# Leaving out the identity matmuls between the products of the level loop in the RWKV scan of a two-layer hybrid backbone

## What is computed

```python
def rwkv7_scan(inputs, s0):
    def step(S, xs):
        r, w, k, v, a, b = xs
        sa = jnp.einsum('bhvk,bhk->bhv', S, a)
        S = S * w[:, :, None, :] + sa[..., None] * b[:, :, None, :] + v[..., None] * k[:, :, None, :]
        return S, jnp.einsum('bhvk,bhk->bhv', S, r)
    return lax.scan(step, s0, inputs)
```

## Time and profile before

| | |
|---|---|
| median of 3 runs | 6901.06 us (6895.18 to 6903.48) |
| span of the profiled execution | 6891.5 us |
| TensorE busy | 4825.8 us (70%) |
| VectorE busy | 4673.2 us (68%) |
| ScalarE busy | 1084.8 us (16%) |
| GpSimd busy | 1818.5 us (26%) |
| RWKV scan, 12 chunks | 839.7 us |

### The profile page before, as it was taken

One profiled execution on the slowest core, in us unless ns is written; L12 is line 12 of the kernel. 1 busy time (PEld: TensorE's weight loads), 2 busy tenths in 40 slices (PEclk: granted clock), 3 DMA queues, 4 the chain that ended last, 5 costly groups with the idle time before them and its releaser, 6 DMA issues.

```text
span 6891.5 us, 63224 instructions
## 1 busy us (share of the span) xinstructions
PE 4825.8 (70%) x17384; PEld 2626.8 (38%) x17384; DVE 4673.2 (68%) x11232; ACT 1084.8 (16%) x2298; POOL 1818.5 (26%) x2660
## 2 busy tenths in 40 slices
PE   8898877869555555555555789987787855555554
PEld 3698454636111111111111269954464411111111
DVE  1554154545999999999987354415463699999977
ACT  1100032211111111111111110002221111111111
POOL 0000000000444444444456100000000144444454
PEclk9899887789677767676777889998768966667777
DMA  5000100001999999999999600000001399999998
GB/s 203 13 1 1 37 10 22 10 25 58 381 390 361 392 362 390 358 392 354 391 375 420 255 22 1 1 31 11 27 7 40 126 389 359 390 371 378 390 390 363
DMA packets 221384, 1463.98 MB, mean 212 GB/s; under 512 B 24593, under 2 KB 28945, under 8 KB 57233
## 3 DMA queue, kind: packets, MB, share of 16 engines
q0 software_dynamic: 184320, 1342.26, 49.0%
q1 hardware_dynamic: 30848, 113.20, 4.6%
q10 hardware_dynamic: 6032, 6.05, 0.3%
HBM read 1459.31 MB, written 2.10 MB: 212 GB/s over the span
## 4 chain that ended last, share of the span: by engine, by line
DVE 43%; PE 36%; issue 11%; DMA 5%; ACT 2%; POOL 1%; DVEq 1%; POOLq 0%; ACTq 0%; SPq 0%
PE psum L335 36%; DVE arena L1511 11%; DVE u_features L1511 7%; DVE arena L1162 5%; DMA arena<-in_uv,arena 4%; DVE arena L1036 3%; DVE psum L1520 2%; DVE arena L1517 1%; DVE arena L1161 1%; DVE arena L1316 1%; DVE arena L1197 1%; DVE arena L1389 1%; DVE arena L1045 1%; DVE arena L1039 1%; DVE arena L1194 1%
## 5 line engine op out<-in xcount | busy, mean ns | idle before, releaser
L335 PE MATMUL psum<-arena,lora_weights 128*128 128x512 f32 (+2 forms) x1968 | 1465.9, 889 | 1026.1 <-ACT lora_weights L970 992.0
L335 PEld LDWEIGHTS psum<-arena,lora_weights 128*128 128x128 f32 (+1 forms) x1968 | 465.8, 261 | 2042.4 <-ACT lora_weights L970 1612.6
L1511 DVE CUSTOM_DVE_ANT_0 arena<-arena,y_features 128x1024 f32<-128x1024 f32 x800 | 957.6, 1221 | 70.4 <-DMA arena<-in_uv,arena 70.4
L335 PE MATMUL psum<-arena 128*128 128x64 f32 (+5 forms) x7136 | 969.6, 315 | 46.9 <-DVE arena L1316 23.8
L1023 POOL DMA_INDIRECT arena<-in_uv,arena x800 | 829.0, 1036 | 239.3 <-issue 212.3
L335 PEld LDWEIGHTS psum<-arena 128*128 128x128 f32 (+2 forms) x7136 | 829.8, 213 | 129.0 <-ACT arena L894 28.8
L335 PE MATMUL psum<-u_features,lora_weights 128*128 128x512 f32 x640 | 512.7, 947 | 484.6 <-ACT lora_weights L970 482.3
L335 PE MATMUL psum<-u_features,weight_ring 128*128 128x256 f32 (+1 forms) x2368 | 782.3, 493 | 16.5 <-DVE u_features L1042 11.6
L1018 POOL COPY arena<-arena 128x2 uint32 x640 | 246.7, 385 | 1753.7 <-PE psum L335 1655.7
L1511 DVE CUSTOM_DVE_ANT_0 u_features<-u_features,y_features 128x1024 f32<-128x1024 f32 x480 | 575.6, 1219 | 23.6 <-DMA u_features<-in_uv,arena 20.8
L335 PEld LDWEIGHTS psum<-u_features,weight_ring 128*128 128x128 f32 x2368 | 458.4, 194 | 326.2 <-issue 272.6
(11 more groups left out here) (187 smaller groups left out, 5013.7 us busy)
## 6 DMA issues: line engine op xcount, KB each, us to landing
weight_ring<-in_ws SPq DMA_DIRECT2D x202, 512.0 KB, 3.3
arena<-in_uv,arena POOLq DMA_INDIRECT x800, 9.6
u_features<-in_uv,arena POOLq DMA_INDIRECT x480
arena<-in_ln ACTq DMA_DIRECT2D x8, 512.0 KB, 4.9
x_tokens<-in_x SPq DMA_DIRECT2D x1, 2048.0 KB, 13.2
out_x<-x_tokens SPq DMA_DIRECT2D x1, 2048.0 KB, 6.6
consts<-in_cf SPq DMA_DIRECT2D x1, 1674.0 KB, 6.8
x_tokens<-in_ctx SPq DMA_DIRECT2D x1, 1024.0 KB, 8.9
```

What stands on the lines that cost most here:

```text
L335: return pe.matmul(o, w, x, start=first, stop=last, skip_group_check=True)
L1511: dve.tensor_tensor_reduce(out=GB[s][:, 0:D], in0=GB[s][:, 0:D], in1=u, scale=1.0, scalar=0.0, op0=ALU.mult, op1=ALU.add, accum_out=DOT[:, ...
```

## The change

The constant WARM goes from 3 to 0:

```diff
-WARM = 3
+WARM = 0
```

## The result

The changed kernel takes 7088.44 us (median of 4 runs, 7066.28 to 7101.42), the kernel before 6898.12 in the same sessions (6890.65 to 6903.48). The ratio is 1.0269, with a 95% interval from 1.0249 to 1.0289: slower by 2.7%. Forecast were 7080 us and 2.6%. The profiled execution spans 7085.7 us against 6891.5, 194.2 us more.

What follows compares the result with a forecast made beforehand. TensorE was taken to bound the RWKV scan, with its clock deciding the sign: +19.9 us in each of ten chunks (+199), -20 for two last chunks, +179 on 6891.5 gives 7070, plus 9.6 makes 7080 us; range 6980 to 7190.

Steps and rivals of the forecast that it cites:

- up to level 1: RWKV chunks with preparation, level 0 up to the start of level 1's "dT": starts earlier, -2.0 us per chunk.
- level 2: Same chunks: wait unchanged at 3.58 us, "dT" between full and half clock, +1.6 us as the middle of 0 and 3.2.
- levels 3, 4, 5: Same chunks: products at half clock, 10.1 us per level instead of 6.7, +3.4 each, +10.2 us per chunk.
- level 6 and the chunk's end: Same chunks: level 6 with the last group +1.1 us; W, U and out partly at half clock, +9 us.
- The pause: Between levels 1 and 2, TensorE's idle time before "dT" grows from 0.24 to 1.84 us, set by VectorE.
- The clock: TensorE's clock falls in or just after the 1.84 us pause and stays low up to W, U and out.
- The last chunks: Last RWKV chunk of each layer: prepares nothing, no pause opens, clock holds; -10 us each, -20 together.
- the 9.6 us added: Added to the forecast span of 7070 us: the 9.6 us by which the median of 6901.06 exceeded the profiled span.
- the first: Rival, RWKV scan: the clock holds and only the saving remains, -80 us, 6821 us; chance 0.12.
- the second: Rival, RWKV scan: the clock falls but is soon back, after levels 2 and 3; 6874 us, chance 0.06.
- the third: Rival: the clock never returns within the RWKV scan, last chunks slow too; +398 us, 7299 us, chance 0.07.
- the fourth: Rival, whole kernel: nothing measurable, gains and losses would have to cancel; chance 0.01.

## Why the prediction was right

The time, 7088 against 7080, and the chunk lengths, 88.5 to 91.1 us against "84 to 96" and 59.1 and 60.1 against "about 60", came out as forecast. By its steps, as means over the ten chunks with preparation, measured between the starts of the second addition to G in each level (line 1341):

| step | before | after | measured | forecast |
|---|---|---|---|---|
| up to level 1 | 22.9 | 20.5 | -2.4 | -2.0 |
| level 2 | 7.2 | 9.7 | +2.5 | +1.6 |
| levels 3, 4, 5 | 3 x 6.7 | 3 x 10.2 | +10.6 | +10.2 |
| level 6 and the chunk's end | 19.8 | 28.6 | +8.8 | +10.1 |
| sum | | | +19.5 | +19.9 |

- **The pause** opened where it was expected, released by VectorE's X; 1.63 us in the trace, 1.84 forecast. Nothing was saved in level 2.
- **The clock** fell in it or behind it, and in the chunk shown stayed at 0.5 until 425.9 us, inside "out" as in all ten chunks. The forecast had leaned to a return there because "out" begins with 128-column products, ten records in a row. The place fits, the reason is not shown: half of W's records and a third of U's stream 128 columns as well, among 64-column ones, and the clock did not return in them. No run varied the columns alone, so why it stays low for so long is open.
- **Level 2** was undersized by 0.9 us. In six of ten chunks the clock fell so early that the level took 9.9 us or more, in four it took 8.5 to 8.9. The forecast took the middle between a fall ahead of "dT" and one behind it, and the early one was more frequent.
- **The chunk's end** was oversized by about 1.3 us together with level 6. Two records of W that took 0.36 us take 0.62, 1.7 times as long and not twice, and about the last 5 us of "out" are at full clock.
- **The last chunks** gained 9.9 and 10.3 us, forecast 10 each.
- **The remainder** of the span, 194.2 - 174.5 = 19.7 us, lies outside the RWKV scan. 9 us of it are the HGRN scans, 423.0 us where they were 413.7, with the same instructions and a lower granted clock in layer 1 (0.62 against 0.65). The prediction had named up to 20 us either way for it and put zero into the sum. The rest is 5.1 us between the two scans of layer 0, 4.7 between its HGRN scan and layer 1's RWKV scan, and less elsewhere; it is less than executions of one kernel differ by (7066 to 7101 us), and no cause is claimed.
- **From span to time** the 9.6 us added were a mistake: they compare the median with the span of another execution. Each run's time is 1.8 us above its own span (7087.47 against 7085.7 here), so 7.8 us too many were added. With the 19.7 us of the remainder left out and the scan put 4.5 us too high, this makes a forecast 7.4 us below the profiled execution and 8.4 below the median. That it is so close is in part luck.

Of the rivals, the first and the second fell in the trace of the change, the third as well, since the clock comes back in level 1 of every chunk, and the fourth by the 2.7%. The first one's price was borne out by the run with filled pauses. The rule that only a long idle gap between bursts costs the clock (the Trainium skill, "TensorE: Matmul & The Clock Gate", section "Why this matters for your kernels") does not hold for this kernel: between the 64-column products of the levels, pauses of 1.00 us lost it in nine of ten chunks and one of 1.13 us in eight of ten. The section on psum-queue depth-cycling of the Trainium skill's same page, which tells of frequent short idle times between groups of matmuls at which the clock swings, describes the fall better, but not that it then stays at half for 58.0 us in which TensorE is never idle.

## What to carry to other kernels

In this kernel the identity matmuls kept the clock where they stood in the pauses; spread between products that follow each other anyway, they cost their own time (102 us here), and removing them was only right once the pause that they shorten was gone. Look first at why TensorE pauses: here VectorE's preparation stood before the operation that TensorE waited for and could be moved behind it, and that with no identity matmuls gave 123 us, more than filling the pauses (77 us). And look at whether the identity matmuls stand on the path of a stage and keep the clock from falling too little to pay for it, as in the HGRN scan, where leaving them out alone gave 51 us.

## What the runs showed of the hardware that was not expected

- The same program with the same pause keeps its clock in one chunk and loses it in another: behind 1.14 and 1.13 us with one identity matmul per group (66.8 against 92.4 us), and behind 1.7 us in level 0 of the run with the preparation moved (58.0 against 60.5 us). Behind this pause in level 0 the clock fell in all twelve chunks of the kernel before and of the change, but in five of twelve of that run, although TensorE's instructions up to there are those of the change. So the length of a pause did not settle it where it was 1.0 to 1.7 us. The pauses ahead of "dT" of level 2 of 1.63 and 2.15 us cost the clock in all ten chunks.
- The cost of a fall was far more than the pause. 1.9 us more of idle time cost 36 us per chunk, since the clock didn't return for five levels, though TensorE was busy throughout and 12 of every 60 records were 128-column identity matmuls.
- A little of the remedy did nothing: one identity matmul per group gave 7100 us (7081 to 7113), none 7088 (7066 to 7101), three 6898.
